# Recurrence gate products from two-part operands: three single-pass matmuls in place of full float32, with the gate weights split on GpSimd

## The chip, the cores and the metric

One core of a Trainium2 chip runs the whole computation in one launch. The metric is the device time of a launch in microseconds (us), median of the runs; lower is better.

## What is computed

The reference is a two-layer hybrid block over 256 image tokens and 256 context tokens, width 1024, in float32. Each layer projects the normalised tokens by `w_in` and feeds four branches: a short gated convolution, windowed attention, a gated linear recurrence (RG-LRU, both directions) and a conformer convolution. The four are gated, summed and projected, and a SwiGLU network follows. The change touches the recurrence alone:

```
u = _dwconv(r_u, conv_c) + conv_c_b
r = sigmoid(einsum('blnc,ncd->blnd', u, wa) + ba)
i = sigmoid(einsum('blnc,ncd->blnd', u, wx) + bx)
log_a = -8 * softplus(-lam) * r
a = exp(log_a);  b = sqrt(-expm1(2 * log_a)) * (i * u)
h = scan(a, b), forwards and backwards, context first
```

`wa` and `wx` are block diagonal: 8 blocks of 128 by 128 for each direction. For one block n there are so four gate matrices (wa and wx, two directions), each applied to the 128 channels of `u` over all 512 tokens.

## The kernel before

Activations lie transposed: 128 channels on the partitions, tokens on the free axis, 8 rows k of 128 channels. A row of both token sets has 512 columns. Layer 1, the last, needs the context tokens only where the recurrence and the attention read them, so there most rows are 256 columns wide.

**Matmuls in three parts.** The weight stream comes in "slabs" of 1 MB (2048 float32 columns): two output tiles of 128 channels with 8 input rows each. ScalarE copies a slab from `RAW` into `WH`, which rounds it to the reduced type float32r (`high`, two halves of 1024 columns), and VectorE or GpSimd writes the rest `RAW - WH` into `WL` (`low` or `lows`). Activations are split in the same way (`HH`/`HL`, `ZH`/`ZL`). A product is then three matmuls of one pass each: high by high, low by high and high by low (`products`). There are two slab buffers, so that the low part of slab n+2 can't be written before slab n is used up.

**The stage c_in.** It has 8 slabs n = 0 to 7, one for each recurrence block: tile 0 is the recurrence input `ru`, tile 1 the gate input `rg`. TensorE runs `ru_rg(n)` and after it `gates(n-1)`; after the first slab of the next stage (`kv`) it runs `gates(7)`, and then the second slab of `kv`. `gates(n)` has four matmuls of 128 by 128 by 512 in plain float32: the weights lie in row n of `CD` (a load of 2 MB from `in_lruw`, once a layer), the moving operand is the convolved row `u`, in `tmp(n % 2)`; the results go to PSUM banks 4 to 7.

Each engine has its own fixed order in c_in for a turn n:

- VectorE: `front(n)` (four convolution taps into `tmp(n % 2)`, then the first half of the GELU), `drives(n-2)`, `scans(n-2)`, `gelu(n)`, `outputs(n-2)`, `weights(n-1)`, `lows(n+2)` (the low part of slab n+2, both halves), `sums(n-1)`. The low part of the first slab of `kv` is so written in turn 6 and that of the second in turn 7.
- ScalarE: `front(n)` (copies `ru` from PSUM, squares `rg`), `roots(n-2)`, `high` for slab n+2, `gelu(n)` (a Tanh), `decays(n-1)` (eight activations, the first four of which read the gates from PSUM), `z_high(n-2)`.
- GpSimd: nothing in c_in. It writes the low parts of the two slabs 0 and 1 of the kernel ahead of it, in layer 1 the low parts of six half rows of the norm (`norm_low`), and from the slabs of `kv` on it writes the low parts of the weight stream.

In layer 0 VectorE also computes the decay rates (`decay_rates(0)`) just before its turn 0: a chain of small operations of 16 columns on the tile `LT`.

Before gates(n), TensorE waits for the last tap of `u` and for `decays(n-1)` to have read the gates of the turn before; before a slab it waits for its low part. The tiles `ZH`/`ZL` are free during c_in except that the result rows of the recurrence go there, row by row (`z_high`, `z_out`).

Of the kernel before, what the change touches and what calls it, by code (L numbers as in the profile page):

```python
# [79 lines left out]
POOL_WHOLE = ("c_in", "kv", "q", "d_in", "c_out", "b_out", "a_cu", "a_b", "w_out")  # L80
WARM_UP = (2, 3)
# [87 lines left out]
def build(nc, stream, modw, lruw, xT, cT, prm, rope, consts, outT):  # L169
    with ExitStack() as ctx:  # L170
        def sb(name, n, dt=F32):
            return ctx.enter_context(nc.sbuf_tensor(name, [P, n], dt))

        def sem(name):
            return ctx.enter_context(nc.semaphore(name))
# [8 lines left out]
        CD = sb("CD", KC * NT)  # L184
# [94 lines left out]

        def lc(j, n, d):  # L280

            return LC[:, ds(n + (16 * j + 8 * d), 1)]
# [44 lines left out]
        def stage_sems(l):  # L327
# [3 lines left out]
            def st(name, names=""):  # L331
                a[name] = Steps(sem(f"{name}_{l}"), names)
# [23 lines left out]
            st("cf_v", "u0 u1 u2 u3 p")  # L356
            st("ci_a", "r0 r1 i0 i1 t0 t1 a0 a1")
            st("ci_s", "s0 s1")
            st("ci_v", "iu0 iu1 w0 w1")
            st("ci_r", "b0 b1 h0 h1 rec y")  # L360
# [149 lines left out]
        def _(pool):  # L510
# [7 lines left out]
            for s in range(2):  # L518
                for h in range(2):
                    low(0, s, h)  # L520
            runs = [(0, 1, 0)]
# [21 lines left out]
            for first, end, halves in [r for r in runs if r[2]]:  # L543
                if first - 1 in ff_first:
                    first += 1
                for l in range(DEPTH):
                    if l > 0 and first == pair_base(l, "kv") + 1:
                        norm_low(l, "n1", 2)
                end_of = end - (end - 1 in ff_first)
# [19 lines left out]
        def _(pe):  # L569
# [248 lines left out]
            for l in range(DEPTH):  # L818
# [11 lines left out]
                def gates(n):  # L830
                    pe.wait_ge(a["cf_v"].sem, a["cf_v"].at(n, "u3"))
                    if n > 0:
                        pe.wait_ge(a["ci_a"].sem, a["ci_a"].at(n - 1, "i1"))
                    for g in range(4):
                        last = mm(bank(4 + g), CD[:, n * NT + g * P:n * NT + (g + 1) * P], tmp(n % 2), True, True)
                    last.then_inc(a["ci_p"].sem, 1)

                pe.wait_ge(lru_loaded, 16 * (l + 1))
# [139 lines left out]
        def _(act):  # L978
# [163 lines left out]
            for l in range(DEPTH):  # L1142
# [34 lines left out]

                def decays(n):
# [18 lines left out]
                for n in range(KC):  # L1197
                    s, m = n % 2, b + n // 2
                    front(n)
                    if n > 1:  # L1200
                        roots(n - 2)
                    high(m + 1, s)
                    gelu(n)
                    if n > 0:
                        decays(n - 1)
                    if n > 1:
                        z_high(n - 2)
# [1197 lines left out]
```

## Time and profile before

| | us |
|---|---|
| median of 3 runs | 1990.16 (1989.03 to 1990.35) |
| span of the profiled execution, first to last instruction | 1986.4 |
| TensorE busy | 1962.3 (99%) |
| VectorE busy | 1369.2 (69%) |
| ScalarE busy | 907.2 (46%) |
| GpSimd busy | 810.8 (41%) |

The profiled execution has no time of its own beside its span; the median of the runs is 3.8 us more than the span, and that is taken as what lies around it. Matmuls are pipelined, so each is shown longer than the time that it holds the engine; the distance between two starts is what one costs. In rows, PE is TensorE, PEld its weight loads, DVE VectorE, ACT ScalarE and POOL GpSimd. `L571`, `L1489`, `L1492`, `L1495`, `L514` and `L980` are helpers through which most instructions of their engine go, so that rows are told apart by tiles. A row of the timeline gives the start, the length in us, engine, line, operation, tiles and shapes, and with "x3" it merges three instructions that follow each other.

### The profile page before, as it was taken

What the parts mean: (1) busy time and instruction counts of PE and PEld (TensorE: products, weight loads), DVE (VectorE), ACT (ScalarE), POOL (GpSimd) and SP (SyncE); (2) the same over time, 40 slices, a digit from 0 to 9 for tenths busy, and PEclk for the clock granted to TensorE, in tenths of its full rate; (3) what the DMA queues carried; (4) which work ended last, traced back from release to release, by engine and by line L of the source; (5) the groups of instructions that cost most, each with busy time, mean ns of one, the idle gap of its engine ahead of it and who ended that gap; (6) DMA issues with size and microseconds to landing.
All of it is one profiled execution on the core that took longest, in us unless ns stands there. A gap on an engine that the chain in (4) does not pass through costs nothing.

```text
span 1986.4 us, 29293 instructions
## 1 busy us (share of the span) xinstructions
PE 1962.3 (99%) x11038; PEld 1665.0 (84%) x11038; DVE 1369.2 (69%) x2403; ACT 907.2 (46%) x1435; POOL 810.8 (41%) x353
## 2 busy tenths in 40 slices
PE   7999999999999999999999999999999999999998
PEld 5778888888888878878888888777999999999998
DVE  5896444567878868788885444589746888645555
ACT  5787544322222252245222222589955444565444
POOL 1002322343434444344344343400646887454442
PEclk9999999999999999999999999999999999999999
DMA  8222211222222234533554452312423555445453
GB/s 344 80 85 84 87 45 63 85 87 104 85 106 85 106 128 172 208 149 128 203 199 171 176 225 90 142 65 85 149 107 128 191 181 196 175 174 186 179 184 128
DMA packets 38701, 276.25 MB, mean 139 GB/s; under 512 B 4416, under 2 KB 4416, under 8 KB 6336
## 3 DMA queue, kind: packets, MB, share of 16 engines
q1 hardware_dynamic: 38592, 274.77, 37.3%
q8 instruction: 72, 1.18, 0.2%
q14 instruction: 37, 0.30, 0.0%
HBM read 273.70 MB, written 1.05 MB: 138 GB/s over the span
## 4 chain that ended last, share of the span: by engine, by line
PE 90%; DVE 6%; ACT 3%; issue 1%; DMA 1%; POOL 0%; SPq 0%; DVEq 0%; ACTq 0%; POOLq 0%
PE PS L571 89%; DVE PS L1492 1%; ACT WH L980 1%; PE PS L877 1%; DVE PS L1489 1%; ACT HH L980 0%; DVE HL L1492 0%; DVE ZL L1492 0%; DVE X L1492 0%; DMA RAW<-in_stream 0%; ACT PS L980 0%; ACT TMP L980 0%; DVE CD L1489 0%; PE PS L669 0%; DVE S L1492 0%
## 5 line engine op out<-in xcount | busy, mean ns | idle before, releaser
L514 POOL TENSOR_TENSOR WL<-RAW,WH 128x1024 fp32r<-128x1024 f32 (+1 forms) x337 | 801.7, 2397 | 1152.1 <-ACT WH L980 1152.0
L980 ACT ACTIVATE WH<-RAW 128x1024 fp32r<-128x1024 f32 (+1 forms) x416 | 414.7, 1043 | 622.9 <-PE PS L571 574.5
L571 PE MATMUL PS<-HH,WH 128*128 128x512 f32 (+2 forms) x1968 | 689.8, 351 | 4.0 <-issue 1.7
L571 PE MATMUL PS<-HH,WL 128*128 128x512 f32 (+2 forms) x1968 | 671.9, 342 | 0.0
L571 PE MATMUL PS<-HL,WH 128*128 128x512 f32 (+2 forms) x1968 | 669.4, 341 | 0.3 <-DVE HL L1492 0.2
L571 PE MATMUL PS<-ZH,WH 128*128 128x512 f32 (+1 forms) x1312 | 444.4, 339 | 3.4 <-DVE HL L1489 2.6
L571 PE MATMUL PS<-ZH,WL 128*128 128x512 f32 (+1 forms) x1312 | 443.8, 339 | 0.0
L571 PE MATMUL PS<-ZL,WH 128*128 128x512 f32 (+1 forms) x1312 | 441.7, 339 | 0.0
L571 PEld LDWEIGHTS PS<-HH,WH 128*128 128x128 f32 x1968 | 370.0, 188 | 58.5 <-issue 10.3
L571 PEld LDWEIGHTS PS<-HL,WH 128*128 128x128 f32 x1968 | 371.1, 189 | 51.7 <-issue 6.0
L571 PEld LDWEIGHTS PS<-HH,WL 128*128 128x128 f32 x1968 | 370.3, 188 | 45.9
L571 PEld LDWEIGHTS PS<-ZH,WH 128*128 128x128 f32 x1312 | 247.3, 188 | 34.5 <-issue 3.5
L571 PEld LDWEIGHTS PS<-ZH,WL 128*128 128x128 f32 x1312 | 247.4, 189 | 30.0
L571 PEld LDWEIGHTS PS<-ZL,WH 128*128 128x128 f32 x1312 | 246.8, 189 | 30.4 <-issue 0.4
L1492 DVE SCALAR_TENSOR_TENSOR PS<-G,PRM,PS 128x512 f32<-128x512 f32 (+1 forms) x464 | 254.3, 615 | 0.1
L980 ACT ACTIVATE TMP<-PS 128x512 f32<-128x512 f32 (+1 forms) x168 | 82.4, 490 | 99.2 <-PE PS L571 49.8
L1489 DVE TENSOR_TENSOR WL<-RAW,WH 128x1024 fp32r<-128x1024 f32 (+1 forms) x79 | 113.6, 1455 | 16.5 <-ACT WH L980 16.5
L1489 DVE TENSOR_TENSOR TMP<-TMP,PS 128x512 f32<-128x512 f32 (+1 forms) x54 | 30.4, 563 | 136.9 <-ACT TMP L980 122.7
L1489 DVE TENSOR_TENSOR PS<-TMP,PS 128x256 f32<-128x256 f32 (+1 forms) x82 | 45.0, 549 | 82.7 <-ACT TMP L980 71.7
L1492 DVE SCALAR_TENSOR_TENSOR PS<-CD,SILC,PS 128x512 f32<-128x512 f32 x112 | 84.7, 756 | 4.0
L1492 DVE SCALAR_TENSOR_TENSOR PS<-G,SILC,PS 128x512 f32<-128x512 f32 x112 | 84.7, 756 | 4.0
L1492 DVE SCALAR_TENSOR_TENSOR G<-G,PS 128x512 f32<-128x512 f32 (+1 forms) x16 | 8.9, 556 | 94.4 <-ACT G L980 94.4
(200 smaller groups left out, 1694.8 us busy)
## 6 DMA issues: line engine op xcount, KB each, us to landing
RAW<-in_stream SPq DMA_DIRECT2D x200, 1024.0 KB, 4.8
CD<-in_modw SPq DMA_DIRECT2D x22, 1024.0 KB, 7.0
G<-in_modw SPq DMA_DIRECT2D x22, 1024.0 KB, 7.2
RAW<-in_stream SPq DMA_DIRECT2D x8, 768.0 KB, 4.1
CD<-in_lruw SPq DMA_DIRECT2D x2, 2048.0 KB, 11.5
X<-in_xT SPq DMA_DIRECT2D x2, 1024.0 KB, 7.0
S<-in_modw SPq DMA_DIRECT2D x2, 1024.0 KB, 13.0
RAW<-in_modw SPq DMA_DIRECT2D x1, 1024.0 KB, 19.8
```

Of the source, the lines that this page charges most:

```text
L514: nc.gpsimd.tensor_tensor(WL[:, a:b], RAW[:, a:b], WH[:, a:b].bitcast(F32), ALU.subtract)\
L571: return nc.tensor.matmul(out, lhs, rhs, start=start, stop=stop)
L877: last = nc.tensor.transpose(bank(4 + u, P, q * P), PR[u % 2][:, q * P:(q + 1) * P], IDENT)
L980: return nc.scalar.activation(out, in_, f, **kw)
L1489: return V.tensor_tensor(out, x, y, op)
L1492: return V.scalar_tensor_tensor(out, x, sc, y, op0, op1)
```

## The change

- `CD` gets a second name `CDR` at the same place, of type float32r.
- GpSimd gets `gate_weights(l)`: for each of the 8 rows of `CD`, in the order of `GATE_ORDER`, a copy into `ZH` (which rounds), a wait for it, and a subtraction into `ZL`, each of 512 columns. It stands behind the low parts of slabs 0 and 1 in layer 0 and behind `norm_low` in layer 1.
- GpSimd gets `driver_lows(l)`, behind all of `gate_weights(l)`: for n = 0 to 7 a subtraction of 512 columns that writes the low part of `u` into rows 3 or 7 of `CD`.
- ScalarE gets `driver_high(n)`, a copy of `u` (512 columns) that rounds it into rows 2 or 6 of `CD`, between `gelu(n)` and `decays(n-1)`. For n = 0 and 1 it waits until the gate weights of the rows of `CD` that it overwrites are split.
- `gates(n)` on TensorE has 12 matmuls with float32r operands instead of 4 in float32, and waits for the low part of `u` and for the split of its row of gate weights. The wait for the load of `CD` goes from TensorE to GpSimd.

```diff
--- before.py
+++ after.py
@@ -78,6 +78,7 @@
 
 
 POOL_WHOLE = ("c_in", "kv", "q", "d_in", "c_out", "b_out", "a_cu", "a_b", "w_out")
+GATE_ORDER = (0, 2, 3, 6, 7, 1, 4, 5)
 WARM_UP = (2, 3)
 GELU_C = 0.7978845608028654
 GELU_A = 0.044715
@@ -171,6 +172,11 @@
         def sb(name, n, dt=F32):
             return ctx.enter_context(nc.sbuf_tensor(name, [P, n], dt))
 
+        def sb_and_rounded(name, n):
+
+            at = (nc.sbuf_base + 31) // 32 * 32
+            return sb(name, n), nc.alloc_sbuf_tensor_at(name + "R", [P, n], F32R, offset=at)
+
         def sem(name):
             return ctx.enter_context(nc.semaphore(name))
 
@@ -181,7 +187,7 @@
         ZL = sb("ZL", KC * NT, F32R)
         S = sb("S", KC * NT)
         G = sb("G", KC * GW)
-        CD = sb("CD", KC * NT)
+        CD, CDR = sb_and_rounded("CD", KC * NT)
         PADA = sb("PADA", 2 * GW)
         RAW = sb("RAW", 2 * SLAB)
         WH = sb("WH", 2 * SLAB, F32R)
@@ -277,6 +283,11 @@
         def normed(nm):
             return (HH, HL) if nm == "n1" else (ZH, ZL)
 
+        def driver(n):
+
+            at = (2 + 4 * (n % 2)) * NT
+            return CDR[:, at:at + NT], CDR[:, at + NT:at + 2 * NT]
+
         def lc(j, n, d):
 
             return LC[:, ds(n + (16 * j + 8 * d), 1)]
@@ -353,11 +364,15 @@
             again("un_e", " ".join(f"b{t}{c}" for t in range(2) for c in vectors) + " "
                + " ".join(f"r{t}{c}" for t in range(2) for c in vectors))
             both("cf_a", "ru sq th", KC)
-            st("cf_v", "u0 u1 u2 u3 p")
-            st("ci_a", "r0 r1 i0 i1 t0 t1 a0 a1")
-            st("ci_s", "s0 s1")
-            st("ci_v", "iu0 iu1 w0 w1")
-            st("ci_r", "b0 b1 h0 h1 rec y")
+            both("cf_v", "u0 u1 u2 u3 p", KC)
+            both("ci_a", "r0 r1 i0 i1 t0 t1 a0 a1", KC)
+            both("ci_s", "s0 s1", KC)
+            both("ci_v", "iu0 iu1 w0 w1", KC)
+            both("ci_r", "b0 b1 h0 h1 rec y", KC)
+            both("gw_h", "w", KC)
+            both("gw_l", "w", KC)
+            both("cf_h", "u", KC)
+            both("cf_l", "u", KC)
             st("ci_h", "zh")
             st("ci_l", "zl")
             st("ci_p", "gates")
@@ -518,6 +533,27 @@
             for s in range(2):
                 for h in range(2):
                     low(0, s, h)
+            def gate_weights(l):
+
+                gh, gl = L[l]["gw_h"], L[l]["gw_l"]
+                pool.wait_ge(lru_loaded, 16 * (l + 1))
+                if l:
+                    read(pool, l - 1, LAST_OUT)
+                for j, n in enumerate(GATE_ORDER):
+                    nc.gpsimd.tensor_copy(row(ZH, n), row(CD, n)).then_inc(gh.sem, 1)
+                    pool.wait_ge(gh.sem, gh.at(j, "w"))
+                    nc.gpsimd.tensor_tensor(row(ZL, n), row(CD, n), row(ZH, n).bitcast(F32), ALU.subtract).then_inc(gl.sem, 1)
+
+            def driver_lows(l):
+
+                uh, ul = L[l]["cf_h"], L[l]["cf_l"]
+                for n in range(KC):
+                    pool.wait_ge(uh.sem, uh.at(n, "u"))
+                    high, rest = driver(n)
+                    nc.gpsimd.tensor_tensor(rest, tmp(n % 2), high.bitcast(F32), ALU.subtract).then_inc(ul.sem, 1)
+
+            gate_weights(0)
+            driver_lows(0)
             runs = [(0, 1, 0)]
             for l in range(DEPTH):
                 for name, n in STAGES:
@@ -546,6 +582,8 @@
                 for l in range(DEPTH):
                     if l > 0 and first == pair_base(l, "kv") + 1:
                         norm_low(l, "n1", 2)
+                        gate_weights(l)
+                        driver_lows(l)
                 end_of = end - (end - 1 in ff_first)
                 cuts = [pair_base(l, LAST_OUT) + x for l in range(DEPTH) for x in (0, 2)]
                 edges = [first] + [x for x in cuts if first < x < end_of] + [end_of]
@@ -828,14 +866,18 @@
                     slab(i + b, s, [(H, NT), (H, W)], ready=ready, halves=1)
 
                 def gates(n):
-                    pe.wait_ge(a["cf_v"].sem, a["cf_v"].at(n, "u3"))
+                    pe.wait_ge(a["cf_l"].sem, a["cf_l"].at(n, "u"))
+                    pe.wait_ge(a["gw_l"].sem, a["gw_l"].at(GATE_ORDER.index(n), "w"))
                     if n > 0:
                         pe.wait_ge(a["ci_a"].sem, a["ci_a"].at(n - 1, "i1"))
+                    uh, ul = driver(n)
                     for g in range(4):
-                        last = mm(bank(4 + g), CD[:, n * NT + g * P:n * NT + (g + 1) * P], tmp(n % 2), True, True)
+                        wh, wl = row(ZH, n, P, g * P), row(ZL, n, P, g * P)
+                        mm(bank(4 + g), wh, uh, True, False)
+                        mm(bank(4 + g), wh, ul, False, False)
+                        last = mm(bank(4 + g), wl, uh, False, True)
                     last.then_inc(a["ci_p"].sem, 1)
 
-                pe.wait_ge(lru_loaded, 16 * (l + 1))
                 if l > 0:
                     ru_rg(0, 0, (l, "n1", 2))
                 for n in range(1, KC):
@@ -1175,6 +1217,14 @@
                     act.wait_ge(fv.sem, fv.at(n, "p"))
                     fn(seqs(tmp(4, 0, W), C), padded(n, C), ACT.Tanh, scale=GELU_C * GELU_A).then_inc(fa.sem, 1)
 
+                def driver_high(n):
+                    act.wait_ge(fv.sem, fv.at(n, "u3"))
+                    if n > 1:
+                        act.wait_ge(a["ci_p"].sem, n - 1)
+                    else:
+                        act.wait_ge(a["gw_l"].sem, a["gw_l"].at(max(GATE_ORDER.index(x) for x in ((6, 7) if n else (2, 3))), "w"))
+                    fn(driver(n)[0], tmp(n % 2), ACT.Copy).then_inc(a["cf_h"].sem, 1)
+
                 def decays(n):
                     act.wait_ge(a["ci_p"].sem, n + 1)
                     if n > 1:
@@ -1201,6 +1251,7 @@
                         roots(n - 2)
                     high(m + 1, s)
                     gelu(n)
+                    driver_high(n)
                     if n > 0:
                         decays(n - 1)
                     if n > 1:
```

## Rows read from the trace of the kernel before

**Rows 1.** The page: the chain that ended last, by engine.
```profile
PE 90%; DVE 6%; ACT 3%; issue 1%; DMA 1%; POOL 0%; SPq 0%; DVEq 0%; ACTq 0%; POOLq 0%
```

**Rows 2.** Timeline of DVE, layer 0: decay rates, turns 0, 6 and 7.
```profile
47.71 1.64 DVE L1492 SCALAR_TENSOR_TENSOR LT<-LT 128x16 f32<-128x16 f32 x8
...
50.34 2.33 DVE L1492 SCALAR_TENSOR_TENSOR TMP<-G,PRM,TMP 128x512 f32<-128x512 f32 x3
...
128.62 0.54 DVE L1495 TENSOR_SCALAR TMP<-G,PRM 128x512 f32<-128x512 f32 x1
...
136.73 0.69 DVE L1492 SCALAR_TENSOR_TENSOR G<-TMP,PS 128x512 f32<-128x512 f32 x1 [0.56 <-ACT TMP L980]
...
143.35 0.54 DVE L1495 TENSOR_SCALAR TMP<-G,PRM 128x512 f32<-128x512 f32 x1
...
155.54 1.22 DVE L1489 TENSOR_TENSOR WL<-RAW,WH 128x1024 fp32r<-128x1024 f32 x1
```

**Rows 3.** Timeline of PEld: the second slab of kv begins, layer 0, layer 1.
```profile
161.87 0.19 PEld L571 LDWEIGHTS PS<-WH,HH 128*128 128x128 f32 x1 [0.24 <-issue]
...
1392.82 0.19 PEld L571 LDWEIGHTS PS<-WH,HH 128*128 128x128 f32 x1 [0.24 <-issue]
```

**Rows 4.** Timeline of DVE, layer 1: turns 6 and 7.
```profile
1366.76 0.55 DVE L1495 TENSOR_SCALAR TMP<-G,PRM 128x512 f32<-128x512 f32 x1
...
1379.49 0.55 DVE L1495 TENSOR_SCALAR TMP<-G,PRM 128x512 f32<-128x512 f32 x1
...
1388.74 2.35 DVE L1489 TENSOR_TENSOR WL<-RAW,WH 128x1024 fp32r<-128x1024 f32 x2
```

**Rows 5.** Timeline of POOL: first row after c_in (layer 0), last before it (layer 1).
```profile
161.17 4.73 POOL L514 TENSOR_TENSOR WL<-RAW,WH 128x1024 fp32r<-128x1024 f32 x2 [113.74 <-ACT WH L980]
...
1293.72 0.73 POOL L538 TENSOR_TENSOR HL<-S,HH 128x256 fp32r<-128x256 f32 x1 [0.57 <-ACT S L980]
```

**Rows 6.** Timeline of PE, layer 0: the matmuls of gates(0) and some after.
```profile
56.34 3.59 PE L571 MATMUL PS<-TMP,CD 128*128 128x512 f32 x8
...
60.00 0.40 PE L571 MATMUL PS<-HL,WH 128*128 128x512 f32 x1
...
60.48 0.39 PE L571 MATMUL PS<-HH,WH 128*128 128x512 f32 x1
```

**Rows 7.** Timeline of PEld, layer 1: the first weight load of gates(0).
```profile
1303.41 0.30 PEld L571 LDWEIGHTS PS<-TMP,CD 128*128 128x128 f32 x2
```

**Rows 8.** The load of the gate weights: issues and landing.
```profile
L471 SPq DMA_DIRECT2D CD<-in_lruw x2: 328/328/328, 25.0 to 1264.7; - x2
...
DMA to landing us min/median/max: 9.0/11.5/14.0
```

**Rows 9.** Groups of POOL by form: count, busy us, mean ns, idle before.
```profile
L514 POOL TENSOR_TENSOR WL<-RAW,WH 128x1024 fp32r<-128x1024 f32 x325 | 779.7, 2417 | 1114.1 <-ACT WH L980 1114.1
...
L538 POOL TENSOR_TENSOR HL<-S,HH 128x256 fp32r<-128x256 f32 x6 | 4.4, 739 | 3.0 <-ACT S L980 3.0
```

**Rows 10.** Timeline, POOL against DVE, where both are at work.
```profile
909.15 2.39 POOL L514 TENSOR_TENSOR WL<-RAW,WH 128x1024 fp32r<-128x1024 f32 x1 [5.42 <-ACT WH L980]
...
909.87 1.96 DVE L1492 SCALAR_TENSOR_TENSOR ZL<-S,MOD,ZH 128x256 fp32r<-128x256 f32 x1
...
912.53 0.87 DVE L1492 SCALAR_TENSOR_TENSOR ZL<-S,MOD,ZH 128x256 fp32r<-128x256 f32 x2
...
189.25 5.22 POOL L514 TENSOR_TENSOR WL<-RAW,WH 128x1024 fp32r<-128x1024 f32 x2 [8.04 <-ACT WH L980]
...
190.32 4.71 DVE L1489 TENSOR_TENSOR PS<-TMP,CD 128x512 f32<-128x512 f32 x2
```

**Rows 11.** Timeline of ACT: a rounding copy of 512 columns.
```profile
97.72 0.63 ACT L980 ACTIVATE ZH<-TMP 128x512 fp32r<-128x512 f32 x1
```

**Rows 12.** Windows: us, busy (x) of PE, PEld, DVE, ACT, POOL, PEclk, DMA.
```profile
1276.00:1280.00 4.00, 4.00 (x28) 3.77 (x28) 1.83 (x9) 0.89 (x2) 0.00 (x0) 0.84 0.52 209
1280.00:1284.00 4.00, 3.96 (x18) 3.18 (x16) 1.30 (x4) 3.95 (x8) 1.68 (x1) 0.73 0.00 0
```

## The prediction

> **What bounds the kernel now.** I read the page's chain first: 90% of it is TensorE [rows 1], and the table has TensorE busy for 99% of the span. So a microsecond taken from TensorE's work counts in full, and so does each microsecond for which TensorE has to wait for something new. Then the timeline of TensorE at a gate block, for what the change takes away; then GpSimd's timeline and its groups, since the change puts 48 instructions there; then VectorE's timeline in c_in, since its instructions and GpSimd's get in each other's way, which is shown in part 2; last the clock.
>
> Two things are to be seen. In c_in VectorE is nearly as full as TensorE. In layer 0 a turn of it takes 14.73 us (128.62 to 143.35), of which it idles 0.56 [rows 2]; in layer 1 a turn takes 12.73 us without an idle gap, while TensorE, having no wait, reaches the second slab of kv at 1392.8 only 1.7 us after VectorE has written its low part (1388.74 + 2.35) [rows 3, 4]. In layer 0 that margin is 161.9 - 156.8 = 5.1 us [rows 2, 3]. And GpSimd is free in c_in, but only from late on: in layer 0 its earlier work ends at 161.17 - 113.74 = 47.4 us, in layer 1 at 1294.5 [rows 5]. The first gates start at 56.3 and 1303.4 [rows 6, 7]. The load of the gate weights, issued at 25.0 and 1264.7, lands at most 14.0 us later [rows 8], so it holds nobody up.
>
> **Part 1, fewer passes on TensorE.** The eight passes of a float32 gate block run from 56.34; the second float32r matmul after it starts at 60.00, the next but one at 60.48 [rows 6]. So a float32r pass costs 0.24 us, and the block 60.00 - 56.34 - 0.24 = 3.42. Twelve float32r passes cost 2.9, or 2.8 where the distance is 0.23. Saved: 0.6 a block, 16 blocks, **9.6 us**, 4.8 a layer. That is the whole gain.
>
> The Trainium skill (FP8 and Floating Point Precision, TensorE Precision Notes) has true float32 as four passes through the array. By that count a block would cost 16 passes, 3.8 us, and the change would save 4 passes, 0.96 a block or 15 in all. The row has 3.42, and the sum goes by the row.
>
> **Part 2, the first gates wait for GpSimd.** This is the largest term. gates(0) now waits for the low part of u(0), and that subtraction stands on GpSimd behind all sixteen instructions of `gate_weights`. A subtraction costs 2.42 us for 1024 columns and 0.74 for 256 [rows 9]; a straight line through both gives 1.30 for 512 and 0.18 for none. The trace has no copy on GpSimd. It has one input in place of two; its bounds are 0.5 (well under half the column cost) and 1.3 (as dear as the subtraction). I take 0.75, the fixed part and half of the column part. With 0.1 for the wait on its own result a pair costs 2.15 and eight pairs 17 us.
>
> GpSimd isn't alone. A VectorE instruction with two operands in SBUF stands still while a GpSimd subtraction runs: one of 256 columns takes 1.96 us inside GpSimd's 909.15 to 911.54, and 0.87 for two where GpSimd is idle; and two of VectorE's, 4.71 together, take turns with two of GpSimd's, which then last 5.22 where 4.73 is usual [rows 5, 10]. So a VectorE instruction waits out GpSimd's, and costs GpSimd some 0.5 itself.
>
> Layer 0: GpSimd starts at 47.4. VectorE is in the chain of decay rates, a dozen small instructions (eight of them in one row, 1.64 us together) before turn 0 [rows 2]; each now waits for one of GpSimd's, about 0.85 on average, +10 us. Its taps of turn 0, which would end at 52.7 [rows 2], end some 13 later with their own waits, at 66; the half GELU 0.7, ScalarE's Tanh and its new copy at 0.6 each [rows 11], and the subtraction 1.3 bring 69. GpSimd's own path is 47.4 + 17 + 2.5 (taps in between) + 1.3 = 68.2. gates(0) starts at 69.2 in place of 56.3: **+13**.
>
> Layer 1: GpSimd starts at 1294.5, right when VectorE begins turn 0. Beside 17 us of its own it lets in six taps and two low parts of slabs, 5.5 more, then the low part of u(0), 1.3: 1318.3 in place of 1303.4, **+15**. ScalarE's copy is long done by then.
>
> The low part of slab 2, which VectorE writes after turn 0, is late too, but not later than the end of gates(0), in either layer.
>
> The Trainium skill (GPSIMD Engine Reference, 3.1 Elementwise) measures 769 ns for 512 elements in a tight loop of its best case. No row here shows that; with it for the copy the sum would be 0.3 us higher.
>
> **Part 3, the clock after the wait.** TensorE now stands still twice for 13 to 15 us. Where it has little to do ahead of layer 1, the granted clock falls to 0.84 and 0.73 of the full 2.4 GHz in two windows of 4 us [rows 12], a loss of 0.64 + 1.08 = 1.7 us. One such loss for each wait: **+3.4** (bounds 0 and 3 us each).
>
> **Part 4, the rest of c_in.** Each turn adds 1.3 us on GpSimd (part 2's price) and 0.63 on ScalarE [rows 11]. ScalarE's copy falls in between its Tanh and the gates' activations; those had reached VectorE just in time, but VectorE is now the later one, so I cost the copy at nothing; if it is not hidden, 0.6 a turn, 4 a layer at most. The subtraction falls beside VectorE's drives and scans, which read two SBUF operands, and costs it 1.1 a turn (1.3 less what an instruction needs to set out anyway); bounds 0 and 1.3.
> - Layer 0: VectorE's turn grows from 14.2 without idling to 15.3, 0.6 more than now, over six turns 3.6. TensorE wants the low part of the second kv slab 4.8 earlier, the margin was 5.1. So 5.1 - 4.8 - 3.6 = -3.3: 3.3 of the 4.8 are given back, **-1.5** stays.
> - Layer 1: VectorE never idles, so five turns of 1.1 are 5.5: 1.7 - 4.8 - 5.5 = -8.6, all of the gain and 3.8 more: **+3.8**.
>
> After kv TensorE is the bound again, and what it has lost stays lost: nothing behind it speeds up for having been late.
>
> **The sum:** 13 + 15 + 3.4 - 1.5 + 3.8 = 33.7 on a span of 1986.4, so 2020.1, and with the 3.8 us around it **2024 us**, against a median of 1990.16.
>
> **Rivals.**
> - *The port is not what it looks like*: the new GpSimd instructions and VectorE's pass each other without blocking. Then gates(0) start at 47.4 + 17 + 1.3 = 65.7 and 1312.8, +9.4 each; the clock 3.4; layer 0 keeps its 4.8, layer 1 keeps 1.7 (its margin; VectorE's turn stays at 12.73). Sum +15.7: 2006. Against it stands the 1.96 of [rows 10]; for it, that the rows show other shapes. Chance 0.13.
> - *The copy costs as much as the subtraction* (1.3, rounding included): 0.55 more for each of 16 rows, 2032. Nothing in the trace excludes it. Chance 0.16.
> - *The other side, the split is hidden*: GpSimd gets through a pair in (56.3 - 47.4 - 1.3) / 8 = 0.95 us in layer 0 and the same in layer 1, so that TensorE never waits. This decides: above 0.95 a pair the first gates wait, and eight times the excess is lost in each layer. Then what is left is the gain, 4.8 in layer 0 and 1.7 in layer 1, 1984. The subtraction alone is 1.3 by [rows 9], so it would need both operations at half of what the line says. Chance 0.04.
> - That the gates don't run in fewer passes is not one: float32r matmuls of this shape stand beside them at 0.24.
>
> **How the numbers follow.** My case 0.67, the port rival 0.13, the dear copy 0.16, the hidden split 0.04. The range takes in the port rival and the dear copy: 2006 to 2036, the upper end with the clock and ScalarE's copy on their upper bounds. A difference of about 0.2%, 4 us, is what a measurement can tell from none; only the hidden split is below it, and of the other cases a hundredth or two may end inside it: faster 0.04, same 0.02, slower 0.94.
>
> **What would show each step.** Right: GpSimd busy without a gap from 47.4 to about 69 and from 1294.5 to 1318; TensorE's two longest waits, 13 and 15 us, put down to GpSimd's subtraction into `CD`; small VectorE instructions on `LT` at about 1 us; a gate block of 2.8; in layer 1 the waits of late slabs on VectorE's `WL`; a clock below 1 behind each wait. Wrong: a first gate block at its old time; VectorE's turn in layer 1 still at 12.7; a copy on GpSimd of 0.4 us or less.

## The result: 2021.72 us, slower by 1.6%, and the profile after

The changed kernel takes 2021.72 us (2019.86 to 2025.03) against 1989.93 for the kernel before on the same chip, ratio 1.0158 with a 95% interval of 1.0145 to 1.017. The profiled span is 2018.1 us, 31.7 more than before; one traced execution stands for the median to within some 3 us, as the control runs below show.

The page's busy line and its chain, the line that answers to [rows 1]. TensorE has 2 us less of work and is on the chain for 80% in place of 90%; what is new on it is GpSimd, with VectorE and ScalarE around it.

```profile
PE 1960.4 (97%) x11102; PEld 1680.4 (83%) x11102; DVE 1399.5 (69%) x2403; ACT 915.3 (45%) x1451; POOL 875.4 (43%) x401
...
PE 80%; DVE 8%; ACT 6%; POOL 3%; DMA 2%; issue 2%; SPq 0%; DVEq 0%; POOLq 0%; ACTq 0%
```

TensorE's waits after (what for: us in total, times, longest). The first line is the first gates of both layers (10.7 and 11.8) and one later wait of 1.4; the second, GpSimd's low parts of the weight stream, 3.7 of the 5.4 in q of layer 1 and 1.4 ahead of c_in; the third, the low parts that VectorE writes in c_in. `L609` is the helper that was `L571`.

```profile
PE PS L609 <- POOL CDR L553: 23.9, 3, 11.8
...
PE PS L609 <- POOL WL L529: 5.4, 5, 2.2
...
PE PS L609 <- DVE WL L1540: 2.8, 3, 1.6
```

TensorE's timeline at the two waits and at a gate block further on. Rows after 67.40 and 1329.06 lie 0.43 us apart for a matmul, those after 82.69 lie 0.23: a block takes 4.20 (67.40 to 71.60) and 4.78 us right behind the waits and 2.79 (82.69 to 85.48) later, against 3.42 [rows 6].

```profile
67.40 1.22 PE L609 MATMUL PS<-CDR,ZH 128*128 128x512 f32 x2 [10.72 <-POOL CDR L553]
68.42 0.63 PE L609 MATMUL PS<-CDR,ZL 128*128 128x512 f32 x1
...
71.60 0.39 PE L609 MATMUL PS<-HH,WH 128*128 128x512 f32 x1
...
82.69 0.62 PE L609 MATMUL PS<-CDR,ZH 128*128 128x512 f32 x2
...
85.48 0.39 PE L609 MATMUL PS<-HH,WH 128*128 128x512 f32 x1
...
1329.06 1.22 PE L609 MATMUL PS<-CDR,ZH 128*128 128x512 f32 x2 [11.83 <-POOL CDR L553]
```

The windows behind the waits (same columns as [rows 12]): the granted clock is 0.64 and 0.50, close to the lower level of 1.2 GHz, for the first 4 us, and back near 1 in the next.

```profile
67.40:71.40 4.00, 4.00 (x12) 3.20 (x13) 3.20 (x5) 1.16 (x2) 0.00 (x0) 0.64 0.44 186
71.40:75.40 4.00, 4.00 (x19) 3.25 (x18) 1.91 (x4) 3.60 (x6) 1.29 (x1) 1.00 0.00 0
1329.00:1333.00 4.00, 3.94 (x9) 3.14 (x10) 0.00 (x0) 0.00 (x0) 1.24 (x2) 0.50 0.00 0
1333.00:1337.00 4.00, 4.00 (x18) 3.17 (x17) 1.08 (x2) 2.96 (x5) 0.00 (x0) 0.97 0.00 0
```

GpSimd after, first the groups (count, busy us, mean ns), then its timeline where VectorE is in small instructions and where it has its taps. Nothing like the first three existed before.

```profile
L553 POOL TENSOR_TENSOR CDR<-TMP,CDR 128x512 fp32r<-128x512 f32 x16 | 26.2, 1638 | 161.6 <-ACT CDR L1022 161.6
L545 POOL TENSOR_TENSOR ZL<-CD,ZH 128x512 fp32r<-128x512 f32 x16 | 23.9, 1493 | 1.3
L543 POOL CAST ZH<-CD 128x512 fp32r<-128x512 f32 x16 | 14.0, 876 | 0.0
```

```profile
47.37 0.61 POOL L543 CAST ZH<-CD 128x512 fp32r<-128x512 f32 x1
48.06 1.32 POOL L545 TENSOR_TENSOR ZL<-CD,ZH 128x512 fp32r<-128x512 f32 x1
49.32 0.61 POOL L543 CAST ZH<-CD 128x512 fp32r<-128x512 f32 x1
...
57.56 1.07 POOL L543 CAST ZH<-CD 128x512 fp32r<-128x512 f32 x1
58.71 1.59 POOL L545 TENSOR_TENSOR ZL<-CD,ZH 128x512 fp32r<-128x512 f32 x1
...
65.91 1.44 POOL L553 TENSOR_TENSOR CDR<-TMP,CDR 128x512 fp32r<-128x512 f32 x1
```

VectorE after, in the same stretch of layer 0 and in a late turn of layer 1. The eight on `LT` took 1.64 [rows 2] and take 5.26, three taps 3.66 in place of 2.33; an instruction with one operand in PSUM (59.21) takes 0.69 as in [rows 2], also beside GpSimd's subtraction of 58.71. The two scans take 3.38; in the kernel before they take 2.33 in every turn.

```profile
48.05 5.26 DVE L1543 SCALAR_TENSOR_TENSOR LT<-LT 128x16 f32<-128x16 f32 x8
...
55.51 3.66 DVE L1543 SCALAR_TENSOR_TENSOR TMP<-G,PRM,TMP 128x512 f32<-128x512 f32 x3
59.21 0.69 DVE L1543 SCALAR_TENSOR_TENSOR G<-TMP,PS 128x512 f32<-128x512 f32 x1
...
1382.86 0.55 DVE L1546 TENSOR_SCALAR TMP<-G,PRM 128x512 f32<-128x512 f32 x1
...
1387.56 3.38 DVE L1862 TENSOR_TENSOR_SCAN TMP<-PADA,TMP 128x512 f32<-128x512 f32 x2
...
1396.64 0.55 DVE L1546 TENSOR_SCALAR TMP<-G,PRM 128x512 f32<-128x512 f32 x1
```

**Where the time went.** I followed how much later the same instruction of TensorE starts than before. Layer 0: gates(0) 11.3 later; 11.8 behind them; 7.8 at gates(7), since the shorter blocks give 4.0 back; 9.6 at the second slab of kv and 11.6 by 250 us. Up to layer 1 it becomes 13.5. Layer 1: gates(0) 25.7, which is 12.1 of its own; 30.1 at the second slab of kv; 33.8 behind q (1450 us in the kernel before); 31.7 at the end. The second slabs of kv, which answer to [rows 3]:

```profile
171.51 0.19 PEld L609 LDWEIGHTS PS<-WH,HH 128*128 128x128 f32 x1 [2.34 <-issue]
...
1423.24 0.19 PEld L609 LDWEIGHTS PS<-WH,HH 128*128 128x128 f32 x1 [1.26 <-issue]
```

### The profile page after: what moved, and what is told of

The parts are those of the page before. It is cut to its first block, busy times and chain, and to the rows that moved or that the text cites. A ratio compares the mean times of both kernels' runs of the same rounds, so it can differ in the third digit from the quotient of the medians.

```text
span 2018.1 us, 29504 instructions
## 1 busy us (share of the span) xinstructions
PE 1960.4 (97%) x11102; PEld 1680.4 (83%) x11102; DVE 1399.5 (69%) x2403; ACT 915.3 (45%) x1451; POOL 875.4 (43%) x401
## 4 chain that ended last, share of the span: by engine, by line
PE 80%; DVE 8%; ACT 6%; POOL 3%; DMA 2%; issue 2%; SPq 0%; DVEq 0%; POOLq 0%; ACTq 0%
PE PS L609 79%; DVE PS L1543 1%; ACT WH L1022 1%; POOL ZL L545 1%; DMA TMP<-in_modw 1%; ACT S L1022 1%; DVE TMP L1543 1%; PE PS L919 1%; DMA RAW<-in_stream 1%; POOL WL L529 1%; ACT TMP L1022 1%; POOL ZH L543 1%; ACT L1022 1%; ACT HH L1022 1%; DVE S L1543 1%
## 5 line engine op out<-in xcount | busy, mean ns | idle before, releaser
L609 PE MATMUL PS<-HH,WH 128*128 128x512 f32 (+2 forms) x1968 | 684.6, 348 | 9.6 <-POOL WL L529 5.4
L609 PE MATMUL PS<-HH,WL 128*128 128x512 f32 (+2 forms) x1968 | 672.1, 342 | 0.0
L609 PE MATMUL PS<-HL,WH 128*128 128x512 f32 (+2 forms) x1968 | 669.4, 341 | 0.3 <-DVE HL L1543 0.3
L609 PE MATMUL PS<-ZH,WH 128*128 128x512 f32 (+1 forms) x1312 | 445.0, 339 | 3.3 <-DVE HL L1540 2.6
L609 PE MATMUL PS<-ZH,WL 128*128 128x512 f32 (+1 forms) x1312 | 443.9, 339 | 0.0
L609 PE MATMUL PS<-ZL,WH 128*128 128x512 f32 (+1 forms) x1312 | 441.9, 339 | 0.0
L609 PEld LDWEIGHTS PS<-HH,WH 128*128 128x128 f32 x1968 | 370.0, 188 | 63.0 <-POOL WL L529 6.9
L609 PEld LDWEIGHTS PS<-HL,WH 128*128 128x128 f32 x1968 | 371.0, 189 | 48.9 <-issue 2.6
L609 PEld LDWEIGHTS PS<-HH,WL 128*128 128x128 f32 x1968 | 370.3, 188 | 45.8
L609 PEld LDWEIGHTS PS<-ZH,WH 128*128 128x128 f32 x1312 | 247.3, 189 | 34.9 <-issue 3.5
L609 PEld LDWEIGHTS PS<-ZH,WL 128*128 128x128 f32 x1312 | 247.4, 189 | 30.1
L609 PEld LDWEIGHTS PS<-ZL,WH 128*128 128x128 f32 x1312 | 246.9, 189 | 30.4 <-issue 0.4
L553 POOL TENSOR_TENSOR CDR<-TMP,CDR 128x512 fp32r<-128x512 f32 x16 | 26.2, 1638 | 161.6 <-ACT CDR L1022 161.6
## 6 DMA issues: line engine op xcount, KB each, us to landing
CD<-in_lruw SPq DMA_DIRECT2D x2, 2048.0 KB, 12.1
```

The costliest lines, as they stand in the source:

```text
L553: nc.gpsimd.tensor_tensor(rest, tmp(n % 2), high.bitcast(F32), ALU.subtract).then_inc(ul.sem, 1)
L609: return nc.tensor.matmul(out, lhs, rhs, start=start, stop=stop)
```

## Experiments

Each kernel was timed beside the kernel before (1989.9 to 1991.5 in its three-round groups). "Late" is how much later the first gates start than before, less what had been lost ahead of c_in. "Turn" is the distance of VectorE's turns once steady; "0 to 3" the distance of its turns 0 and 3 in layer 1.

| kernel | median us | ratio (95%) | late, layer 0 / 1 | turn, layer 0 / 1 | 0 to 3 |
|---|---|---|---|---|---|
| before | 1989.93 | | 0 / 0 | 14.63 / 12.73 | 32.8 |
| after | 2021.72 | 1.0158 (1.0145 to 1.017) | 11.2 / 12.1 | 15.12 / 13.8 | 46.7 |
| e_order | 2010.89 | 1.0094 (1.0073 to 1.0114) | 4.0 / 0.7 | 15.11 / 13.82 | 39.3 |
| e_warm | 2019.03 | 1.0141 (1.0121 to 1.0161) | 11.2 / 12.2 | 15.12 / 13.8 | 44.8 |
| e_twice | 2032.77 | 1.0209 (1.0187 to 1.0232) | 11.2 / 12.1 | 15.57 / 14.85 | 47.2 |
| e_gain | 1987.76 | 0.9979 (0.9969 to 0.9989) | 0 / 0 | 14.06 / 12.73 | 32.0 |
| e_plain | 2026.38 | 1.0173 (1.0153 to 1.0194) | 11.2 / 12.1 | 14.73 / 13.8 | 47.5 |
| e_layer0 | 2003.88 | 1.0059 (1.004 to 1.0078) | 11.2 / 0 | 15.12 / 12.73 | 32.8 |
| e_vlow | 2005.47 | 1.007 (1.0054 to 1.0087) | 7.3 / 0.7 | 14.67 / 13.33 | 38.2 |
| e_early | 2004.38 | 1.007 (1.0053 to 1.0086) | 5.9 / 0 | 14.66 / 13.33 | 36.6 |
| e_copies | 1998.45 | 1.0038 (1.0023 to 1.0052) | 2.8 / 0 | 15.12 / 13.8 | 32.6 |
| e_nopool | 2002.83 | 1.006 (1.0043 to 1.0077) | 1.9 / 1.5 | 14.66 / 13.33 | 37.7 |

**The two controls.** The kernel before, unchanged:

> The kernel before once more, for a second trace. In its first trace TensorE goes through q of layer 1 without a wait, while in the changed kernel and in all four experiments so far it loses about 4 us there, also in the one that adds nothing on GpSimd. Theory (the weight stream there follows VectorE's last low part in c_in, which is late against TensorE in all of them and was not before): again no wait in q, VectorE's turns of 12.73. Rival (run to run): 2 us or more of waits in q of layer 1 here too. The time is 1990 to 1992.

1989.90 us, ratio 0.9991 (0.998 to 1.0001). No wait in q of layer 1, turns of 12.73, so the loss in q is not chance. But its trace is 5.0 us longer than the first: 2.4 at the start, 1.5 with a lower clock near 950 us. The same 1.5 stands in the changed kernel's trace, so that part of the 13.5 is not the change's. The changed kernel again:

> The changed kernel once more beside the other two, for a second trace: 2020 to 2024 us. What repeats in both traces is the change's (VectorE's turns of 15.1 and 13.8, its scans of 3.4 for two, the first gates 11 to 12 late in both layers, some 4 us lost in q of layer 1), and what doesn't is not (a lower clock at the first matmuls of the second half of layer 0's last stages, 1.5 us).

2021.23 us, ratio 1.0158 (1.0141 to 1.0175). First gates 11.2 and 12.1 late, turns 15.11 and 13.8 and the loss in q (4.0 us) repeat; near 950 us nothing is lost. One thing more does not repeat: between the second slab of kv and 250 us the first trace lost 2 us in layer 0, most of it at a granted clock of 0.59 in the window 172 to 176 us behind a wait of 1.9 us, and here TensorE is 9.8 later than before at that slab and 9.4 by 250, with the clock at 1.00.

**e_gain: the gain alone.** The first norm's rows stand in for weights and u, so the gates are those of other data.

```diff
-                        last = mm(bank(4 + g), CD[:, n * NT + g * P:n * NT + (g + 1) * P], tmp(n % 2), True, True)
+                        wh, wl = row(HH, n, P, g * P), row(HL, n, P, g * P)
+                        mm(bank(4 + g), wh, row(HH, n), True, False)
+                        mm(bank(4 + g), wh, row(HL, n), False, False)
+                        last = mm(bank(4 + g), wl, row(HH, n), False, True)
```

> The kernel before, with twelve float32r matmuls in a gate block, whose operands are rows of the first norm that have long been there: nothing is added on GpSimd or ScalarE, and the gates are those of other data. Theory (part 1: 0.6 us a block; layer 0 has the margin to keep 4.8, layer 1 keeps what VectorE lets it, 1.7 to 3): 1983.5 us (1981.5 to 1985.5), a block takes 2.8. Rival (float32r passes in a block of four banks don't run at 0.24): 1990.

1987.76 us: 3.7 less than before, not 8. Layer 0 keeps all of its part, TensorE is 5.7 earlier at the second slab of kv. In layer 1 TensorE gets ahead by 2.8 more, but VectorE's turns stay at 12.73, and q takes 6.1 us back, 3.1 of them in waits for the weight stream's low parts that the kernel before hasn't; behind q it is 3.3 later against before than it was ahead of c_in. So the change, free of its costs, could give 4 us, and all of that in layer 0.

**What takes the time in q.** The traces show the chain, though no run was made to move it alone. Behind the last low part that it writes, VectorE has two instructions on `S` and then a low part `ZL`, for which ScalarE waits before its last gates' activations; only behind those does ScalarE round the next slab, which GpSimd's low part and TensorE then want. GpSimd's first two low parts of kv start at about the same moment. In the kernel before VectorE begins its two instructions 1.1 us ahead of them, is hardly touched, and ScalarE doesn't wait; in e_gain and in the changed kernel GpSimd begins first, the two take 5.7 us in place of 1.29, ScalarE stands still for 2.8 and 3.4 us, and TensorE's longest wait for GpSimd's low parts in q is 2.2 us in both. First the kernel before, then e_gain with its line of waits, then the changed kernel:

```profile
1391.02 1.29 DVE L1492 SCALAR_TENSOR_TENSOR S<-S 128x512 f32<-128x512 f32 x2
1392.12 5.11 POOL L514 TENSOR_TENSOR WL<-RAW,WH 128x1024 fp32r<-128x1024 f32 x2 [97.67 <-ACT WH L980]
...
1385.66 5.20 POOL L514 TENSOR_TENSOR WL<-RAW,WH 128x1024 fp32r<-128x1024 f32 x2 [95.65 <-ACT WH L983]
1385.70 5.70 DVE L1495 SCALAR_TENSOR_TENSOR S<-S 128x512 f32<-128x512 f32 x2
1391.82 1.28 ACT L983 ACT_TABLE_LOAD   x1 [2.83 <-DVE ZL L1492]
PE PS L571 <- POOL WL L514: 3.1, 2, 2.2
...
1422.43 5.79 POOL L529 TENSOR_TENSOR WL<-RAW,WH 128x1024 fp32r<-128x1024 f32 x2 [6.04 <-ACT WH L1022]
1423.09 5.68 DVE L1543 SCALAR_TENSOR_TENSOR S<-S 128x512 f32<-128x512 f32 x2
1429.18 1.28 ACT L1022 ACT_TABLE_LOAD   x1 [3.42 <-DVE ZL L1540]
```

All eleven traces with another c_in in layer 1 have it (ScalarE waits 2.8 to 3.7 us, q loses 3 to 6); the three with the old one (before, e_before, e_layer0) don't.

**e_plain: the gain taken away, the costs kept.**

```diff
-                        mm(bank(4 + g), wh, uh, True, False)
-                        mm(bank(4 + g), wh, ul, False, False)
-                        last = mm(bank(4 + g), wl, uh, False, True)
+                        last = mm(bank(4 + g), wh.bitcast(F32), tmp(n % 2), True, True)
```

> The changed kernel with the gate products back in plain float32: four matmuls in a block instead of twelve, on the rounded gate weights and u. All work and all waits of the change stay (GpSimd's split, ScalarE's copies); the two small products are left out of the result. Theory (VectorE's turn, lengthened by GpSimd's work, sets the pace of c_in in both layers, so that what TensorE saves in a block is worth little there): of the 9.6 us of part 1 at most 4 come back, 2022 to 2026 us. Rival (TensorE sets the pace, as the sum took it for most of layer 0): all 9.6 us come back, 2031 us.

2026.38 us, between the two theories: of 9.6 us, 4.7 to 5.2 are worth something (by the ratios, 3). In layer 0 the turn is then 14.73 and TensorE never catches up, so there it is TensorE that sets the pace; the theory holds for layer 1, where TensorE loses 17.3 us in c_in with the long blocks and 16.5 with the short ones. Both experiments say that about half of the work taken from TensorE, or more, was not on the path.

**e_layer0: one layer alone.** `gate_weights`, `driver_lows`, `driver_high` and the new gate block only in layer 0.

> The change in layer 0 alone; layer 1 has its gates in plain float32 and nothing new on GpSimd and ScalarE. Theory (by the starts of TensorE's instructions in the changed kernel's trace, 11.6 us later behind layer 0's c_in than before, 13.5 by layer 1): 2003 to 2005 us. Rival (both layers lose the same, half of 31.6): 2007.5.

2003.88 us, as forecast: layer 0 costs 12.8, layer 1 the other 17 to 19. Its trace has no wait in q of layer 1, so the loss there belongs to the changed c_in of that layer.

**e_order: u(0) ahead of five of the eight rows.**

```diff
-GATE_ORDER = (0, 2, 3, 6, 7, 1, 4, 5)
+GATE_ORDER = (0, 2, 3, 1, 6, 7, 4, 5)
...
-            gate_weights(0)
-            driver_lows(0)
+            def gate_operands(l):
+                gate_weights(l, 0, 3)
+                driver_lows(l, [0])
+                gate_weights(l, 3, KC)
+                driver_lows(l, range(1, KC))
```

> GpSimd splits the gate weights of rows 0, 2 and 3, then writes the low part of u(0), then splits the other five rows and goes on as in the changed kernel (2021.7 us). Theory (the first gates wait because u(0) stands behind all sixteen instructions): in layer 0 three pairs end near 54, u(0) and its rounding near 58, so gates(0) start near 59 instead of 67.4 (before 56.1); in layer 1 they start within 1 to 2 us of the place that they had before. About 20 of the 23.4 us of the two waits go, 2001 us (1998 to 2005). Rival (what costs is GpSimd at work beside VectorE, in whatever order): VectorE's turn 0 is held up all the same, gates(0) in layer 0 stay later than 64 and the time stays above 2012.

2010.89 us, a miss by 10. The waits did go, as the theory has it: TensorE's at 60.51 is 3.5 us, the one at 1311.75 is 0.4.

```profile
60.51 0.86 PE L614 MATMUL PS<-CDR,ZH 128*128 128x512 f32 x2 [3.46 <-POOL CDR L554]
...
1311.75 0.73 PE L614 MATMUL PS<-CDR,ZH 128*128 128x512 f32 x2 [0.41 <-POOL CDR L554]
```

But the time came back only in part. In layer 1 the first gates are 11.4 us less late than in the changed kernel, and TensorE is only 6.6 better off at the second slab of kv and 4.3 behind q. VectorE tells why: its first three turns take 39.3 us in place of 32.8, since its taps and low parts now run beside the split of the remaining rows, and from there each turn is 1.1 longer. VectorE's timeline in turns 0 and 1 of layer 1, where three taps take 3.70 and 4.38:

```profile
1304.37 3.70 DVE L1548 SCALAR_TENSOR_TENSOR TMP<-G,PRM,TMP 128x512 f32<-128x512 f32 x3
...
1309.34 3.43 DVE L1545 TENSOR_TENSOR WL<-RAW,WH 128x1024 fp32r<-128x1024 f32 x2
...
1313.57 4.38 DVE L1548 SCALAR_TENSOR_TENSOR TMP<-G,PRM,TMP 128x512 f32<-128x512 f32 x3
```

**e_twice: the suspected cost doubled.** The low part of u(n) is written twice for n > 0, the second time after a wait for the first.

> The changed kernel with GpSimd's low part of u(n) written twice for n = 1 to 7. Theory (each costs VectorE's turn about 1.1, and VectorE has no margin left in either layer): seven turns a layer get 1.1 to 1.4 longer, most of it on the path, 2032 to 2038 us. Rival (the subtraction passes beside VectorE for nothing and only has to be in time for the gates, with some 2 us to spare): 2021 to 2023.

2032.77 us, 11.1 to 11.5 above the changed kernel. The turn in layer 1 goes from 13.8 to 14.85, and the whole of it stands in the scans: 2.33, 3.38 and 4.46 for none, one and two subtractions.

```profile
1376.70 4.46 DVE L1867 TENSOR_TENSOR_SCAN S<-S 128x512 f32<-128x512 f32 x2
...
1378.01 2.07 POOL L558 TENSOR_TENSOR CDR<-TMP,CDR 128x512 fp32r<-128x512 f32 x1
```

In layer 0 the second one costs a turn 0.46 only.

**e_warm: the clock.**

```diff
                 def gates(n):
+                    if n == 0:
+                        for _ in range(WARM_GATES[l]):
+                            mm(bank(4), HH[:, 0:P], HH[:, 0:NT], True, True)
```

> The changed kernel, with 43 and 46 idle matmuls of 512 columns (about 0.24 us each) into bank 4 ahead of gates(0), which fill the wait for its operands; gates(0) overwrite that bank. Theory (part 3 of the prediction: the granted clock drops during the wait and takes 1.3 to 1.7 us from the work behind each): the clock stays at 1.00 behind both waits, and the time is 2.5 to 3.5 us below the changed kernel's 2021.7, 2018.7. Rival (the clock comes back at once and the loss is elsewhere): 2021.7 or a little more.

2019.03 us. The first four microseconds behind the waits are at full clock:

```profile
68.00:72.00 4.00, 3.83 (x17) 3.13 (x18) 3.34 (x5) 0.48 (x1) 0.11 (x1) 1.00 0.77 266
...
1326.80:1330.80 4.00, 3.99 (x17) 3.29 (x18) 0.00 (x0) 0.90 (x2) 1.19 (x1) 1.00 0.02 4
```

From the first weight load of gates(0) to that of gates(1) it takes 13.76 and 11.17 us, in the changed kernel 15.07 and 13.17 (second trace 15.48 and 12.86): 3.3 to 3.4 for both. The time is 2.2 to 2.7 lower by the medians, where 2.5 to 3.5 was expected, and the intervals of the ratios (1.0121 to 1.0161, 1.0145 to 1.017) overlap a little, so the two windows carry this more than the median.

**e_vlow: VectorE writes the low part of u.** On top of e_order.

```diff
+                def driver_low(n):
+                    dve.wait_ge(a["cf_h"].sem, a["cf_h"].at(n, "u"))
+                    high, rest = driver(n)
+                    tt(rest, tmp(n % 2), high.bitcast(F32), SUB).then_inc(a["cf_l"].sem, 1)
...
                     gelu(n)
+                    driver_low(n)
```

> The order of e_order (2010.9 us), but VectorE writes the low part of u(n) itself, right behind gelu(n), and GpSimd doesn't. Theory (a subtraction of GpSimd costs VectorE's turn 1.1 us in layer 1, by its turns of 12.73 before and 13.83 in e_order; VectorE's own of 512 columns costs half of its 1.2 for 1024, 0.6): VectorE's turn in layer 1 is 13.35 us, some 0.5 less in six or seven turns, and little in layer 0: 2007 us (2005 to 2009). Rival (the 1.1 is the subtraction's own latency and not the shared path): the turn stays at 13.8 or grows, and the time is 2011 or more.

2005.47 us, 5.4 less than e_order. The turn is 13.33; the instruction is booked with 0.69, and the scans are back at 2.33:

```profile
1370.95 2.33 DVE L1870 TENSOR_TENSOR_SCAN TMP<-PADA,TMP 128x512 f32<-128x512 f32 x2
...
1386.83 0.69 DVE L1543 TENSOR_TENSOR CDR<-TMP,CDR 128x512 fp32r<-128x512 f32 x1
```

So handing this subtraction to an idle GpSimd costs VectorE 1.1 a turn, and doing it itself 0.6.

**e_copies: only the copies.** The eight subtractions on the weights are left out, and the third product uses the high part again.

> The changed kernel without GpSimd's eight subtractions on the gate weights in each layer: only the rounding copies stay, and the third product of a block uses the high part again. A row then takes GpSimd 0.70 to 0.88 us, below the 0.95 at which the prediction's last rival has the first gates wait no longer. Theory of that rival: gates(0) at their old start in both layers, and of the two waits nothing is left, yet the low parts of u stay: 2002 us. Theory of a shared path (VectorE is held up by the copies too): gates(0) in layer 0 are 3 to 4 us later than before, in layer 1 by 1 or less; 2003 to 2007 us. If the subtraction's own path is what blocks and the copy doesn't, VectorE's small instructions on LT take 1.6 us for eight again.

1998.45 us, below both. The eight copies take 4.52 us, 0.57 each, well below the 0.95 at which the prediction saw the waits vanish. In layer 1 they do; in layer 0 gates(0) are still 2.8 late, since the copies hold VectorE's chain up as well (3.73 for the eight on `LT`, against 1.64), and it is VectorE's u(0) that comes last. I had set layer 1 too high: there VectorE's turn 0 takes 8.4 us in place of 6.5, but turns 1 and 2, in which it idled before, make that good (turns 0 to 3 in 32.6).

```profile
48.03 4.52 POOL L543 CAST ZH<-CD 128x512 fp32r<-128x512 f32 x8
...
49.26 3.73 DVE L1541 SCALAR_TENSOR_TENSOR LT<-LT 128x16 f32<-128x16 f32 x8
```

**e_early: split while GpSimd is idle.** On top of e_vlow, three rows ahead of slab 1's low parts in layer 0, two rows ahead of them in layer 1.

> e_vlow (2005.5 us) with part of the gate weights split while GpSimd idles: rows 0, 2 and 3 of layer 0 ahead of the low parts of slab 1, rows 0 and 2 of layer 1 ahead of the low parts of the first odd slab of c_in, the rest where it was. Theory (each pair of GpSimd beside VectorE's decay chain and turns 0 and 1 delays VectorE, and with it the first gates and all that follows): gates(0) in layer 0 within 3 us of their old start instead of 9, and 1 to 2 us less in layer 1: 2000 us (1997 to 2002). Rival (VectorE's own slower start is due to something else, such as its new wait for ScalarE's copy): 2004 or more.

2004.38 us, the same ratio as e_vlow: a miss. GpSimd was idle at 39 us, VectorE was not. It was writing the last rows of the first norm, and they were held up in turn: three scalings that take 1.28 in e_vlow take 2.65, two low parts 2.23 in place of 0.88, and TensorE waits 3.2 us for them, so that the first gates come 1.3 later than in e_vlow.

```profile
38.80 2.65 DVE L1553 SCALAR_TENSOR_TENSOR S<-X,AMP,TMP 128x256 f32<-128x256 f32 x3
...
38.98 0.78 POOL L541 CAST ZH<-CD 128x512 fp32r<-128x512 f32 x1 [14.90 <-DMA CD<-in_lruw]
...
41.37 2.23 DVE L1553 SCALAR_TENSOR_TENSOR HL<-S,MOD,HH 128x256 fp32r<-128x256 f32 x2
```

**e_nopool: nothing new on GpSimd.** On top of e_vlow, ScalarE rounds the weights and VectorE subtracts.

```diff
+                    if n < 2:
+                        gate_low(3 * n, 3 + 5 * n)
                     driver_low(n)
```

> e_vlow (2005.5 us) with the gate weights off GpSimd as well: ScalarE rounds the rows (in layer 0 all eight before its turn 0, in layer 1 three in turn 0 and five in turn 1), VectorE subtracts (three rows in turn 0, five in turn 1). GpSimd has nothing in c_in, as before the change. Theory (a GpSimd instruction beside VectorE costs VectorE more than the same subtraction done by itself, 0.6 us each): gates(0) in layer 0 some 3 us later than before instead of 9, and behind turn 3 of layer 0 VectorE 4 to 5 us earlier than in e_vlow; in layer 1, where e_vlow's three first turns took 38.2 us in place of 32.9, about 5 are added again: 2001 us (1998 to 2003). Rival (the subtractions cost VectorE the same wherever they run): 2004 to 2007.

2002.83 us, the best version of the full change, at the upper edge of the theory. Layer 0 does what was expected: gates(0) 1.9 late, and by 250 us TensorE is 1.1 ahead of the kernel before. ScalarE's eight copies took 4.26 us, which it had to spare (its idle time before its turn 0 goes from 5.2 to 1.6), and the eight on `LT` behind them 1.64:

```profile
43.94 4.26 ACT L999 ACTIVATE ZH<-CD 128x512 fp32r<-128x512 f32 x8
...
48.19 1.64 DVE L1534 SCALAR_TENSOR_TENSOR LT<-LT 128x16 f32<-128x16 f32 x8
```

Nearly all of its loss is in layer 1, 5.8 in c_in and 5.9 in q: VectorE was full there before, and has 5 us of subtractions and 0.6 a turn more. A version with this form in layer 0 and plain float32 in layer 1 was not run; by these traces it would end 1 to 2 us below the kernel before, less than can be measured.

## Why the prediction was right, and where it was not

The sum was 33.7 and the difference of the medians is 31.8 (30.3 for the second pair, e_after and the kernel before beside it). Term by term, from the first two traces:

| step | predicted | measured |
|---|---|---|
| gate block | 2.8 | 2.79 |
| first gates, layer 0 | +13 | +11.2 |
| first gates, layer 1 | +15 | +12.1 |
| clock behind both | +3.4 | +3.3 |
| rest of layer 0 | -1.5 | -1.0 |
| rest of layer 1 | +3.8 | +2.5 in c_in, +3.7 in q |

(The rests are what is left of 11.6 by 250 us, and of 30.1 - 13.5 and 33.8 - 13.5, less the first gates and 1.3 and 2.0 for the clock. These terms add up to 31.8. The 1.9 that come on between 250 us and layer 1, 1.5 of it near 950 us and not the change's, and the 2.1 that come back between 1450 us and the end, nearly cancel.)

That the sum came so close is in part luck. The first gates were set 5 us too high and the rest of layer 1 1.3, and the 3.7 in q, which the sum hadn't, filled the gap. The -1.0 for the rest of layer 0 belongs to one execution: 2 us of it went by behind c_in and did not in the second trace, where the rest is -3.9; at the second slab of kv, the place for which the prediction worked it out, it is -3.0 and -3.5, so that term was too high as well. And the 3.8 us taken to lie around the span are 1.8 in every later traced run; the first trace seems to be of an execution 2 us faster than the median.

- **Part 1** is right for the new block: 12 passes at 0.23. The old one was read a little low: the eight rows of a float32 block lie 0.43 apart, and from three matmuls ahead of a block to the sixth behind it takes 0.67 less after (5.54 and 4.87), not 0.6. Eight rows at 0.43 are also sixteen passes at 0.215, so the prediction's aside with four passes a matmul isn't contradicted by its 3.42; what doesn't fit there is the 0.24 taken for each pass. What the blocks are worth did not hold: e_gain puts the whole gain at 3.7, not 9.6. The prediction booked 4.8 in each layer and gave most of it back in part 4, so the sum didn't suffer.
- **Part 2, the size.** Undisturbed, the copy takes 0.61 (I took 0.75, between 0.5 and 1.3) and the subtraction 1.3, as the straight line said; a pair starts every 1.95 in place of 2.15. Beside VectorE a pair takes 2.3 in layer 0 (47.37 to 65.91 for eight) and 2.5 in layer 1, where I had 2.15 and let in 5.5 us of VectorE's work. That is the 2 and 3 us by which the two terms are too large: the price of the pair, and a taking of turns counted too dear. In layer 0 the prediction had two paths to the first gates, 69 by VectorE and 68.2 by GpSimd. VectorE's was far off: its taps of turn 0 end at 59.2 (55.51 + 3.66), 6.5 late and not 13, and ScalarE's copy at 61.1. GpSimd's own path decides, 67.4.
- **Part 2, the mechanism** is confirmed: small instructions on `LT` went from 0.2 to 0.66 each (I said 1), and moving instructions from GpSimd to VectorE makes VectorE's turn shorter (e_vlow). The Trainium skill (GPSIMD Engine Reference, 1. Specifications) has GpSimd's SBUF interfaces shared with VectorE, contended by VectorE instructions with two SBUF inputs or in a two-port mode; the trace agrees, the scans and taps are stretched and the instruction with a PSUM operand is not. The first rival (no blocking, 2006) is out.
- **Part 3** is right in size and shown by e_warm, with the clock at the lower level behind each wait.
- **Part 4, VectorE's turn**: 1.1 predicted, 1.1 in layer 1 and 0.5 net in layer 0 (14.63 to 15.12). There too it is 1.1 on the bare turn, which e_gain shows at 14.06 where the prediction took 14.2. It stands in the scans, as the prediction placed it.
- **The step that failed**: "After kv TensorE is the bound again". In layer 1 it isn't: 3.7 us more are lost in q, with waits for the weight stream's low parts. It happens in every kernel with a changed c_in in layer 1, e_gain included, and in none with the old one (before, e_before, e_layer0), so it needs neither GpSimd's new work nor a late first gate. The traces put it down to part 2's own mechanism at a place where the prediction did not look: GpSimd's old work on the slabs of kv falls beside VectorE's last instructions of c_in, 5.7 us in place of 1.29, and ScalarE and then TensorE wait for them (see e_gain). In layer 0 the same two are stretched too (2.88 and 2.86), but in the second trace TensorE loses nothing by it.
- **A threshold that failed**: 0.95 us a pair does not decide whether the first gates wait. e_copies is well under it and they are 2.8 late in layer 0, because u(0) itself comes late from VectorE. I had counted VectorE's hold-up in the sum and forgotten it in the rival.
- **What the terms hide**: they add up here because both layers end up with VectorE as the bound. Taken one at a time they don't. Layer 1's wait of 12.1 was not the price of the order alone: with the wait gone (e_order) some 5 us of it came back as longer VectorE turns, and 2 more in q.

## What to carry to other kernels

An idle engine is free only if it shares nothing with the busy one: here each 1.3 us subtraction on GpSimd took 1.1 us from VectorE, which does it in 0.6. Before work is moved off the engine that is full, ask which engine is full next (in layer 1 VectorE had no idle time in its turn), since work taken from the first is then worth little and work added to the second counts in full. Look also at where the last work of the stage meets the first of the next: there 1 us of shift put two engines beside each other and cost 3 to 6. And take a wait apart by an experiment before it is priced: a wait that stands in front of a second full engine hides that engine's delay.

## What the runs showed of the hardware that I had not expected

- GpSimd's plain copy, with a single SBUF input, also holds VectorE up: 3.73 us for eight 16-column instructions that take 1.64 alone (e_copies).
- Who pays depends on the size of VectorE's instruction. Beside the 16-column chain on `LT` GpSimd keeps its 0.61 and 1.32, and VectorE alone pays (0.2 to 0.66 each); against taps of 512 columns both do (GpSimd's copies of 0.61 become 1.07 or 1.6).
- A GpSimd copy of 512 float32 columns with rounding costs 0.61 us, 0.57 in a row of eight; ScalarE's rounding copy 0.53 in a row of eight.
- Behind the same wait of 2.6 us near 950 us the granted clock was 0.67 and 0.71 in a stretch of 4 us in some executions and stayed at 1.00 in others, for one and the same kernel: the second trace of the kernel before and the first of the changed one have it, the other two don't. It cost 1.5 us each time. Behind a wait of 1.93 us at the second slab of kv it was 0.59 in the changed kernel's first trace and 1.00 in e_order's.
